# Dense expert gates: one 128-column product per token in place of two of 64, and the second half's gates fetched back in two parts

## The chip, the cores and the metric

The kernel runs on one core of one Trainium2 chip. The metric is the device time of one execution in microseconds (us), taken as the median of several runs; lower is better. Tensors are f32; TensorE (PE) multiplies a stationary 128x128 operand by a moving one and writes into the eight PSUM banks of 512 f32 columns; VectorE (DVE), ScalarE (ACT) and GpSimd (POOL) do the rest, and SyncE (SP) issues most loads.

## The reference, cut to what matters

Two transformer blocks; the change lies in the last part, the layer of 16,384 experts addressed by product keys (128 first keys times 128 second keys). Each of 512 tokens picks 16 experts for each of 8 heads:

```
sc, idx = top_k(query . sub_keys)            # 16 first and 16 second keys per head
top_sc, pos = top_k(sums of pairs)           # 16 pairs per head -> expert = first*128 + second
gate = softmax(top_sc)
act  = gelu(u_tab[expert] . h)               # 128 chosen experts per token
y    = sum(gate * act * v_tab[expert])
```

## The kernel before, in words

Of the four blocks of 128 tokens the kernel handles the first two sparsely: each of 256 "rows" is an indirect DMA on POOL's queue (L1279) that fetches one expert's up and down vector (8 KB) for each of 128 tokens, 1 MB in all; DVE takes the dot product (L3549), ACT the gelu and the weight (L2679, L2681), and DVE adds the weighted down vector (L3561). A row's place is fetched again only once the row before it in that place was added.

The other 256 tokens are handled densely, over all experts. There are 256 *items* of 512 KB, loaded by SP into four buffers (`raws`, L1081), each as soon as the item four before is done. An up item j (`up_unit`, L2017) gives the pre-activations of the 128 experts with second key j, and ACT writes their gelu into `weights[:, j % 64, :]` (`activate`, L2659). A down item m (`down_unit`, L2032) multiplies `weights[:, m % 64, :]`, by then multiplied by the gates, with its down vectors and accumulates in PSUM banks 0 to 3. Only 64 of the 128 second keys fit in `weights` at a time, so the work has two halves. The gate of (token, first key, second key) is found by a scatter done as a matrix product: for a token, `one_first` holds a one-hot row of the first key for each of its 128 (head, choice) entries, `one_second` the one-hot row of the second key times the gate, and their product is the 128x128 gate matrix.

`STEPS` is the order that all engines follow:
- 64 up items (second keys 0 to 63);
- the **gate stage**: 32 steps (`NGATE`) of 8 tokens (`GTOK`). DVE builds `one_first` for 8 tokens (L3512) and `one_second` for four of them with one instruction each (L3516), POOL `one_second` for the other four (L1293); PE makes two products per token (L2044), columns 0 to 63 into one bank and 64 to 127 into the next. DVE multiplies the first bank into `weights` (`gate_weights`, L3528); ACT copies the second to SBUF (`keep_gates`, L2667) and stores it in DRAM (`weights_dram`, L2670), since the second half's gelu values don't exist yet;
- the **mix stage**: 128 items, a down item of the first half and an up item of the second in turn;
- the **back stage**: DVE multiplies the gates fetched back into `weights` (`later_weights`, L3537), 32 times 128x512. SP loads them with `load_gates` (L1091) into `LOADS` = 4 buffers: the first four in the middle of the mix stage, the others behind the item load that ends it, each when a buffer is free. The first down item of the second half waits for all 32 (`down_unit`, L2029);
- the **last stage**: 64 down items.

Rows are spread over the steps by `row_step`: 10 in the gate stage, 120 in the mix stage, 2 in the back stage, 60 in the last. Each engine issues in its program's order: in a step DVE does `one_hots` of it, `gate_weights` of the step before, the addition of the rows of the step before, then the dot products of its own; ACT does the gelu of the step before, `keep_gates` of the step before, then its rows' weights. PE may write a bank once `bank_out` says that it was read.

## Time and profile before

| | us |
|---|---|
| median of 3 runs | 3542.27 |
| range of the runs | 3540.53 to 3545.55 |
| the profiled execution, its own time | 3543.44 |
| its span, first to last instruction | 3541.7 |
| PE busy / DVE busy / POOL busy / ACT busy | 3341.8 / 2201.1 / 1880.8 / 905.8 |

PE's matmul and weight load are separate rows (PE and PEld). Every f32 product appears as two weight loads and two matmuls. The mean granted clock of TensorE over the span is 0.949 of full speed. A row of a timeline gives start, length from the first start to the last end of the group, engine, line, operation and count, and in brackets the idle time before it with what ended it. "DMA share" is the mean busy share of the core's 16 DMA engines; queue q0 is POOL's, q1 is SP's.

### The profile page before, as it was taken

To read this page: it belongs to the slowest core of one execution; us is meant where nothing else is said; L and a number is where in the kernel's file an instruction comes from. 1 tells how busy PE (TensorE), PEld (TensorE's weight loads), DVE (VectorE), ACT (ScalarE), POOL (GpSimd) and SP (SyncE) were. 2 spreads that over 40 slices of the span, in tenths; PEclk is the share of its full clock that TensorE was granted. 3 is DMA by queue.
4 is the path that set the end of the run, shared out by engine and by line. 5 is a ranking of instruction groups with operands and counts; after the bars stand their busy time and mean duration, and the time that the engine had idled before them with its cause. 6 is when DMAs were issued, how large, how long until landed. Compare 5 with 4: busy or idle time off the path is not lost.

```text
span 3541.7 us, 39029 instructions
## 1 busy us (share of the span) xinstructions
PE 3341.8 (94%) x14292; PEld 2517.4 (71%) x14292; DVE 2201.1 (62%) x3653; ACT 905.8 (26%) x1952; POOL 1880.8 (53%) x1072
## 2 busy tenths in 40 slices
PE   8999999999999999999999999997899988996898
PEld 5779778886857888688776677766899655663433
DVE  5764443337674333589367767899655896566765
ACT  4564431112174111201123413222211221111111
POOL 3544269997104999698775472222577333342420
PEclk9999999999999999999999999999755999998999
DMA  4430022222302222234312127777622899999996
GB/s 161 166 130 1 24 86 102 97 107 83 131 36 72 95 95 95 83 110 143 104 72 95 37 89 300 279 267 279 220 86 103 333 364 417 381 412 375 384 417 268
DMA packets 117764, 628.72 MB, mean 178 GB/s; under 512 B 12889, under 2 KB 13017, under 8 KB 62041
## 3 DMA queue, kind: packets, MB, share of 16 engines
q1 hardware_dynamic: 72496, 343.07, 26.3%
q0 software_dynamic: 36864, 268.45, 19.4%
q10 hardware_dynamic: 8232, 14.95, 1.1%
q8 instruction: 103, 1.69, 0.2%
q14 instruction: 69, 0.56, 0.0%
HBM read 607.55 MB, written 18.87 MB: 177 GB/s over the span
## 4 chain that ended last, share of the span: by engine, by line
PE 72%; DVE 11%; DMA 10%; issue 3%; ACT 2%; POOL 1%; DVEq 0%; ACTq 0%; POOLq 0%; SPq 0%
PE bank L1447 13%; PE bank L1448 13%; PE bank L1449 13%; PE bank L2017 6%; PE bank L2032 6%; PE bank L2044 6%; DMA residual<-in_peer_ut 5%; DMA residual<-in_peer_vd 3%; DVE arena L3549 1%; PE bank L1893 1%; PE bank L1875 1%; PE bank L1761 1%; DVE squares L3381 1%; PE bank L1394 1%; PE bank L1639 1%
## 5 line engine op out<-in xcount | busy, mean ns | idle before, releaser
L1449 PE MATMUL bank<-split_arena 128*128 128x512 f32 x1776 | 696.3, 392 | 0.0
L1279 POOL DMA_INDIRECT arena<-in_peer_uv,rstd x181 | 261.8, 1446 | 624.3 <-DVE weight_ring L3561 325.3
L1186 POOL TENSOR_TENSOR split_arena<-weight_ring,ones 128x1024 fp32r<-128x1024 f32 x204 | 505.1, 2476 | 155.1 <-PE bank L1449 99.2
L1447 PE MATMUL bank<-split_arena 128*128 128x512 f32 x1392 | 546.6, 393 | 5.4 <-DVE split_normed L2908 2.5
L1448 PE MATMUL bank<-split_arena 128*128 128x512 f32 x1392 | 542.5, 390 | 0.0
L2017 PE MATMUL bank<-normed,residual 128*128 128x256 f32 x2048 | 483.3, 392 | 55.1 <-ACT arena L2659 37.1
L1188 POOL TENSOR_TENSOR split_arena<-weight_ring,split_arena 128x1024 fp32r<-128x1024 f32 x204 | 520.1, 2550 | 16.0
L2032 PE MATMUL bank<-residual,arena 128*128 128x512 f32 x1024 | 468.7, 604 | 47.3 <-DVE arena L3537 41.4
L2017 PEld LDWEIGHTS bank<-normed,residual 128*128 128x128 f32 x2048 | 395.9, 196 | 162.0 <-issue 59.8
L2032 PEld LDWEIGHTS bank<-residual,arena 128*128 128x128 f32 x1024 | 190.4, 192 | 288.2 <-issue 238.6
L1449 PEld LDWEIGHTS bank<-split_arena 128*128 128x128 f32 x1776 | 334.4, 188 | 73.1
L1155 POOL TENSOR_TENSOR split_arena<-weight_ring,split_arena 128x1024 fp32r<-128x1024 f32 x54 | 129.5, 2407 | 401.9 <-ACT split_arena L2170 349.9
L1447 PEld LDWEIGHTS bank<-split_arena 128*128 128x128 f32 x1392 | 261.9, 188 | 68.0 <-issue 8.1
L1448 PEld LDWEIGHTS bank<-split_arena 128*128 128x128 f32 x1392 | 261.7, 188 | 55.1 <-issue 1.2
L3549 DVE CUSTOM_DVE_ANT_0 arena<-arena,branch 128x1024 f32<-128x1024 f32 x181 | 220.2, 1220 | 30.9 <-DMA arena<-in_peer_uv,rstd 30.7
L1447 PE MATMUL bank<-split_normed,split_arena 128*128 128x512 f32 x560 | 223.5, 399 | 4.9 <-DVE split_arena L3185 3.8
L1448 PE MATMUL bank<-split_normed,split_arena 128*128 128x512 f32 x560 | 222.1, 397 | 0.0
L2679 ACT ACTIVATE row_gelu<-dots 128x1 f32<-128x1 f32 x256 | 51.5, 201 | 648.1 <-DVE dots L3549 648.0
L1279 POOL DMA_INDIRECT weight_ring<-in_peer_uv,rstd x75 | 103.0, 1373 | 171.3 <-DVE branch L3561 96.5
L1293 POOL TENSOR_SCALAR branch<-arena,masks 128x128 f32<-128x128 f32 x128 | 152.4, 1201 | 55.5 <-PE bank L2044 50.6
L3561 DVE SCALAR_TENSOR_TENSOR branch<-arena,row_gelu,branch 128x1024 f32<-128x1024 f32 x84 | 107.8, 1283 | 105.3 <-ACT row_gelu L2681 104.8
L2211 ACT ACTIVATE squares<-squares 128x512 f32<-128x512 f32 x64 | 40.4, 632 | 486.6 <-DVE squares L2823 486.6
(508 smaller groups left out, 5476.9 us busy)
## 6 DMA issues: line engine op xcount, KB each, us to landing
residual<-in_peer_ut SPq DMA_DIRECT2D x128, 512.0 KB, 7.5
residual<-in_peer_vd SPq DMA_DIRECT2D x128, 512.0 KB, 11.0
weight_ring<-in_w_up SPq DMA_DIRECT2D x32, 1024.0 KB, 4.8
weight_ring<-in_w_down SPq DMA_DIRECT2D x32, 1024.0 KB, 4.8
weight_ring<-in_w_in SPq DMA_DIRECT2D x32, 1024.0 KB, 4.9
weight_ring<-in_ada_w SPq DMA_DIRECT2D x24, 1024.0 KB, 4.8
weight_ring<-in_w_in_a SPq DMA_DIRECT2D x12, 1024.0 KB, 6.6
weight_ring<-in_w_out SPq DMA_DIRECT2D x12, 1024.0 KB, 6.9
```

Source lines behind the costliest of these rows:

```text
L1155: pool.tensor_tensor(lo, raw(u)[:, :, h * P:(h + 1) * P], f32(hi), ALU.subtract).then_inc(split_ready, 1)
L1186: pool.tensor_tensor(hi, part, bc_mid(ones[:], DT), ALU.mult).then_inc(split_hi, 1)
L1188: pool.tensor_tensor(lo, part, f32(hi), ALU.subtract).then_inc(split_ready, 1)
L1279: pool.indirect_dma_start(row_places[i][0], None, a["peer_uv"], bass.IndirectOffsetOnAxis(ap=experts[n][:, c:c + 1], axis=0)).then_inc(row ...
L1293: m = pool.tensor_scalar(one_second[q % 2][:, x, :], iota_key, index_t[b][:, 1, at:at + 1], index_t[b][:, 2, at:at + 1], ALU.is_equal, ALU ...
L1447: pe.matmul(psum[t.bank][:], hi, a_hi[k], start=first, stop=False)
L1448: pe.matmul(psum[t.bank][:], lo, a_hi[k], start=False, stop=False)
L1449: return pe.matmul(psum[t.bank][:], hi, a_lo[k], start=False, stop=last)
L2017: m = pe.matmul(psum[t.bank][:, 0:DENSE], blk(raws[n % RAWS], k), H[:, k, DENSE:], start=k == 0, stop=k == DT - 1)
L2032: x = pe.matmul(psum[2 * b + c][:], blk(weights[:, m % WHALF, :], b), raws[n % RAWS][:, 512 * c:512 * (c + 1)], start=m == 0, stop=m == NK ...
L2044: m = pe.matmul(psum[t.bank][:, x * WHALF:(x + 1) * WHALF], one_first[q % 2][:, x, :], one_second[q % 2][:, x, half * WHALF:(half + 1) * W ...
L3549: dve.tensor_tensor_reduce(row, row, h_tok[:, n, :], 1.0, 0.0, ALU.mult, ALU.add, dots[:, r % RING8:r % RING8 + 1]).then_inc(row_dot, 1)
```

## The change

All 128 second keys of a token come from one product of 128 columns, so a bank now holds four tokens, both halves. `one_second` is built as plain one-hots by one DVE instruction for six tokens (POOL keeps two, still multiplied by the gate); ACT then multiplies the six by their gates in place (`scale_ones`) before PE uses them. ACT's `keep_gates` copies the second half out of both banks and signals `gate_read`; DVE's `gate_weights` waits for that and multiplies the first half out of both banks. The stored gates come back in two parts of 32 second keys: part 0 is loaded with one load per item from item 132 on and multiplied in by DVE in 32 steps of the mix stage (`back_at`), part 1 in the back stage. There are eight buffers of half the size.

```diff
-LOADS = 4
+LOADS = 8
+BACKS = 2
+BACK_J = WHALF // BACKS
+POOL_HOT = 2
...
+        BACK_ITEM = WHALF + WHALF + 4
+        back_at = {MIX_AT + WHALF + 3 + q: q for q in range(NGATE)}
...
-            def load_gates(q):
+            def load_gates(n):
-                if q == 0:
+                part, q = divmod(n, NGATE)
+                if n == 0:
                     full(sp, gate_tiles[NGATE - 1][0])
                     for x in gate_stored:
                         sp.wait_ge(x, 16 * NGATE // 2)
-                if q >= LOADS:
-                    sp.wait_ge(gate_used, q - LOADS + 1)
-                sp.dma_start(gate_back[q % LOADS], weights_dram[q]).then_inc(gate_landed[q % LOADS], 16)
+                if n >= LOADS:
+                    sp.wait_ge(gate_used, n - LOADS + 1)
+                sp.dma_start(gate_back[n % LOADS], weights_dram[q][:, part * BACK_J * GTOK:(part + 1) * BACK_J * GTOK]).then_inc(
+                    gate_landed[n % LOADS], 16)
...
-                elif n == 2 * WHALF:
-                    for q in range(LOADS):
-                        load_gates(q)
+                elif BACK_ITEM <= n < BACK_ITEM + NGATE + LOADS:
+                    load_gates(n - BACK_ITEM)
                 elif n == 3 * WHALF + RAWS - 1:
-                    for q in range(LOADS, NGATE):
+                    for q in range(NGATE + LOADS, BACKS * NGATE):
                         load_gates(q)
                     sp.dma_start(H[:, :, :], x_dram).then_inc(x_back, 16)
...
-                for x in range(GTOK // 2, GTOK):
+                for x in range(GTOK - POOL_HOT, GTOK):
...
-                    pe.wait_ge(gate_used, NGATE)
+                    pe.wait_ge(gate_used, BACKS * NGATE)
...
+                pe.wait_ge(scaled_hot, q + 1)
...
                 for x in range(GTOK):
-                    for half, t in enumerate(gate_tiles[q]):
-                        m = pe.matmul(psum[t.bank][:, x * WHALF:(x + 1) * WHALF], one_first[q % 2][:, x, :],
-                                      one_second[q % 2][:, x, half * WHALF:(half + 1) * WHALF], start=True, stop=True)
+                    t = gate_tiles[q][2 * x // GTOK]
+                    m = pe.matmul(blk(psum[t.bank], x % (GTOK // 2)), one_first[q % 2][:, x, :], one_second[q % 2][:, x, :],
+                                  start=True, stop=True)
...
             def keep_gates(q):
-                t = gate_tiles[q][1]
                 if q >= 2:
                     act.wait_ge(gate_stored[q % 2], 16 * (q // 2))
-                full(act, t)
-                act.activation(gate_out[q % 2].rearrange("p (j t) -> p j t", t=GTOK), psum[t.bank][:].rearrange("p (t j) -> p j t", t=GTOK),
-                               ACT.Copy).then_inc(bank_out[t.bank], 1)
-                have(act, t)
+                full(act, gate_tiles[q][0])
+                dst = gate_out[q % 2].rearrange("p (j t) -> p j t", t=GTOK)
+                for x, t in enumerate(gate_tiles[q]):
+                    m = act.activation(dst[:, :, x * GTOK // 2:(x + 1) * GTOK // 2],
+                                       psum[t.bank][:].rearrange("p (t j) -> p j t", j=NKEY)[:, WHALF:, :], ACT.Copy)
+                m.then_inc(gate_read, 1)
+                act.wait_ge(gate_read, q + 1)
                 act.dma_start(weights_dram[q], gate_out[q % 2]).then_inc(gate_stored[q % 2], 16)
+            def scale_ones(q):
+                b, t = divmod(q, NGATE // 2)
+                act.wait_ge(vector_hot, q + 1)
+                for x in range(GTOK - POOL_HOT):
+                    one = one_second[q % 2][:, x, :]
+                    m = act.activation(one, one, ACT.Copy, scale=index_t[b][:, 2, GTOK * t + x:GTOK * t + x + 1])
+                m.then_inc(scaled_hot, 1)
...
+                if kind == "gate":
+                    scale_ones(v)
                 if s and STEPS[s - 1][0] == "gate":
                     keep_gates(STEPS[s - 1][1])
...
-                for x in range(GTOK // 2):
-                    at = GTOK * t + x
-                    m = dve.tensor_scalar(one_second[q % 2][:, x, :], iota_key, index_t[b][:, 1, at:at + 1],
-                                          index_t[b][:, 2, at:at + 1], ALU.is_equal, ALU.mult)
-                m.then_inc(vector_hot, 1)
+                own = GTOK - POOL_HOT
+                dve.tensor_tensor(one_second[q % 2][:, 0:own, :], bc_mid(iota_key, own), bc_last(index_t[b][:, 1, GTOK * t:GTOK * t + own], NKEY),
+                                  ALU.is_equal).then_inc(vector_hot, 1)
...
-                w = weights[:, :, GTOK * q:GTOK * (q + 1)]
-                full(dve, t)
-                dve.tensor_tensor(w, w, psum[t.bank][:].rearrange("p (t j) -> p j t", t=GTOK), ALU.mult).then_inc(bank_out[t.bank], 1)
+                dve.wait_ge(gate_read, q + 1)
+                for x, t in enumerate(gate_tiles[q]):
+                    w = weights[:, :, GTOK * q + x * GTOK // 2:GTOK * q + (x + 1) * GTOK // 2]
+                    dve.tensor_tensor(w, w, psum[t.bank][:].rearrange("p (t j) -> p j t", j=NKEY)[:, 0:WHALF, :],
+                                      ALU.mult).then_inc(bank_out[t.bank], 1)
...
-                w = weights[:, :, GTOK * q:GTOK * (q + 1)]
-                dve.wait_ge(gate_landed[q % LOADS], 16 * (q // LOADS + 1))
-                dve.tensor_tensor(w, w, gate_back[q % LOADS].rearrange("p (j t) -> p j t", t=GTOK), ALU.mult).then_inc(gate_used, 1)
+                w = weights[:, part * BACK_J:(part + 1) * BACK_J, GTOK * q:GTOK * (q + 1)]
+                dve.wait_ge(gate_landed[n % LOADS], 16 * (n // LOADS + 1))
+                dve.tensor_tensor(w, w, gate_back[n % LOADS].rearrange("p (j t) -> p j t", t=GTOK), ALU.mult).then_inc(gate_used, 1)
...
                 for r in rows_at[s]:
                     dot_row(r)
+                if s in back_at:
+                    later_weights(0, back_at[s])
```

## Rows read from the trace of the kernel before

**Rows 1.** The page: PE's granted clock in tenths, 40 slices of 88.5 us

```profile
PEclk9999999999999999999999999999755999998999
```

**Rows 2.** Busy time by stretch: start:end, length, engines, clock, DMA share, GB/s

```profile
2531.00:2749.00 218.00, 218.00 (x1024) 218.00 (x1023) 110.46 (x209) 22.98 (x49) 157.76 (x136) 0.50 0.28 96
...
3012.00:3018.00 6.00, 6.00 (x14) 4.85 (x15) 0.00 (x0) 0.00 (x0) 0.00 (x0) 0.50 0.65 264
3018.00:3024.00 6.00, 6.00 (x21) 3.74 (x21) 3.76 (x5) 1.27 (x5) 1.68 (x1) 0.99 0.43 123
...
3060.00:3240.00 180.00, 177.16 (x584) 107.64 (x584) 110.52 (x136) 29.77 (x117) 74.00 (x47) 1.00 1.02 414
3245.00:3286.00 41.00, 0.00 (x0) 0.00 (x0) 25.70 (x39) 1.23 (x5) 2.28 (x2) 0.52 0.88 313
3286.00:3296.00 10.00, 9.88 (x18) 4.30 (x19) 8.35 (x12) 1.99 (x8) 3.92 (x3) 0.74 0.45 162
3296.00:3500.00 204.00, 201.09 (x489) 85.02 (x488) 142.17 (x173) 30.49 (x117) 61.67 (x52) 1.00 1.01 415
```

**Rows 3.** Timeline of one gate step, and the stage's first and last instruction

```profile
2523.87 1.22 DVE L3512 TENSOR_TENSOR mem_keys<-arena,masks 128x1024 f32<-128x1024 f32 x1 [3.19 <-ACT masks L2143]
...
2564.83 7.03 PE L2044 MATMUL bank<-branch,mem_values 128*128 128x64 f32 x32
...
2565.68 1.22 DVE L3512 TENSOR_TENSOR mem_keys<-arena,masks 128x1024 f32<-128x1024 f32 x1
...
2566.82 1.11 DVE L3516 TENSOR_SCALAR branch<-arena,masks 128x128 f32<-128x128 f32 x4
...
2750.23 6.16 PE L2032 MATMUL bank<-residual,arena 128*128 128x512 f32 x8 [0.87 <-DVE arena L3528]
```

**Rows 4.** Like instructions (timeline, groups, two lines' instructions with min/median/max ns, gate stage)

```profile
2517.29 1.05 PE L1949 MATMUL bank<-mem_values,arena 128*128 128x128 f32 x8
2124.75 2.45 ACT L2586 ACTIVATE normed<-normed,ada 128x128 f32<-128x128 f32 x8
2558.86 1.28 DVE L3561 SCALAR_TENSOR_TENSOR weight_ring<-weight_ring,row_gelu 128x1024 f32<-128x1024 f32 x1
2572.51 1.22 DVE L3549 CUSTOM_DVE_ANT_0 arena<-arena,branch 128x1024 f32<-128x1024 f32 x1
L2659 ACT ACTIVATE arena<-bank 128x256 f32<-128x256 f32 x128 | 47.9, 375 | 217.6 <-PE bank L2017 217.5
L3451 DVE TENSOR_TENSOR weight_ring<-iota,rstd 128x256 f32<-128x256 f32 x4 | 1.7, 424 | 0.1
L1293 POOL TENSOR_SCALAR branch<-arena,masks x124: 780/795/2862, 2531.8 to 2739.2; 128x128 f32<-128x128 f32 x124
L3549 DVE DVE_READ_ACCUMULATOR2_ANT dots<- x10: 78/82/84, 2527.2 to 2723.8; 128x1 f32 x10
```

**Rows 5.** Mix stage: longest wait; item loads before, first and after the four gate loads

```profile
3012.00 6.70 PE L2017 MATMUL bank<-normed,residual 128*128 128x256 f32 x16 [12.53 <-DMA residual<-in_peer_ut]
DMA to landing us min/median/max: 3.6/11.3/11.3
2984.88 0.82 SPq L1091 DMA_DIRECT2D mem_keys<-gate_half  x2
DMA to landing us min/median/max: 19.0/22.6/23.8
```

**Rows 6.** DMA queues between 3060 and 3240 us: packets, MB, share of 16 engines

```profile
q0 software_dynamic: 6671, 48.62, 65.1%
q1 hardware_dynamic: 7097, 25.86, 36.2%
```

**Rows 7.** Timeline of the back stage: start, first wait, first products after

```profile
3245.32 1.29 DVE L3537 TENSOR_TENSOR arena<-arena,mem_keys 128x512 f32<-128x512 f32 x2 [5.88 <-ACT arena L2659]
...
3252.58 1.32 DVE L3537 TENSOR_TENSOR arena<-arena,mem_keys 128x512 f32<-128x512 f32 x2 [3.61 <-DMA mem_keys<-gate_half]
...
3286.12 14.32 PE L2032 MATMUL bank<-residual,arena 128*128 128x512 f32 x27 [41.37 <-DVE arena L3537]
```

More of the change, by code:

```diff
@@ L785, in build @@
         gate_out = [work_a, work_b]
-        gate_back = [k[:, i * SEQ:(i + 1) * SEQ] for k in keys_t for i in range(2)]
+        gate_back = [k[:, i * UNIT_N:(i + 1) * UNIT_N] for k in keys_t for i in range(4)]
         index_t = [masks[:, 3 * i:3 * i + 3, :] for i in range(2)]
@@ L907, in build @@
         pool_hot = sem("pool_one_hot_ready")
+        scaled_hot = sem("one_hot_scaled")
+        gate_read = sem("gate_banks_copied")
         gate_stored = [sem(f"gate_half_stored{i}") for i in range(2)]
@@ L2025, in down_unit @@
                         free(pe, t)
-                    for t, _ in gate_tiles[NGATE - 2:]:
+                    for t in gate_tiles[NGATE - 2] + gate_tiles[NGATE - 1]:
                         have(pe, t)
                 elif m == WHALF:
-                    pe.wait_ge(gate_used, NGATE)
+                    pe.wait_ge(gate_used, BACKS * NGATE)
                 for b in range(2):
@@ L3513, in one_hots @@
                                   ALU.is_equal)
-                for x in range(GTOK // 2):
-                    at = GTOK * t + x
-                    m = dve.tensor_scalar(one_second[q % 2][:, x, :], iota_key, index_t[b][:, 1, at:at + 1],
-                                          index_t[b][:, 2, at:at + 1], ALU.is_equal, ALU.mult)
-                m.then_inc(vector_hot, 1)
+                own = GTOK - POOL_HOT
+                dve.tensor_tensor(one_second[q % 2][:, 0:own, :], bc_mid(iota_key, own), bc_last(index_t[b][:, 1, GTOK * t:GTOK * t + own], NKEY),
+                                  ALU.is_equal).then_inc(vector_hot, 1)
             def gate_weights(q):
-                t = gate_tiles[q][0]
                 if q == 0:
@@ L3525, in gate_weights, with later_weights @@
                         have(dve, x)
-                w = weights[:, :, GTOK * q:GTOK * (q + 1)]
-                full(dve, t)
-                dve.tensor_tensor(w, w, psum[t.bank][:].rearrange("p (t j) -> p j t", t=GTOK), ALU.mult).then_inc(bank_out[t.bank], 1)
-            def later_weights(q):
+                dve.wait_ge(gate_read, q + 1)
[3 more added lines that the diff above has]
+                                      ALU.mult).then_inc(bank_out[t.bank], 1)
+            def later_weights(part, q):
+                n = part * NGATE + q
                 if q == 0:
-                    for x in u_tiles[NKEY - 2:]:
+                    end = WHALF + (part + 1) * BACK_J
+                    for x in u_tiles[end - 2:end]:
                         have(dve, x)
-                w = weights[:, :, GTOK * q:GTOK * (q + 1)]
-                dve.wait_ge(gate_landed[q % LOADS], 16 * (q // LOADS + 1))
-                dve.tensor_tensor(w, w, gate_back[q % LOADS].rearrange("p (j t) -> p j t", t=GTOK), ALU.mult).then_inc(gate_used, 1)
+                w = weights[:, part * BACK_J:(part + 1) * BACK_J, GTOK * q:GTOK * (q + 1)]
+                dve.wait_ge(gate_landed[n % LOADS], 16 * (n // LOADS + 1))
+                dve.tensor_tensor(w, w, gate_back[n % LOADS].rearrange("p (j t) -> p j t", t=GTOK), ALU.mult).then_inc(gate_used, 1)
             def dot_row(r):
@@ L3578, in _ @@
                     for q in range(LOADS * v, LOADS * (v + 1)):
-                        later_weights(q)
+                        later_weights(1, q)
                 elif s == MIX_AT:
```

## The prediction

> **What bounds the kernel now.** I read the page first, then busy time by stretch, then timelines of the places that the edit touches. The page shows PE's clock at half for three slices in a row [rows 1]; by stretch that is the gate stage, 218 us with PE busy for all of it at 0.50, the 1.2 GHz level, while DVE and ACT are busy 110 and 23 us [rows 2]. So PE bounds this stage: a step of 8 tokens is 32 matmul records in 7.03 us [rows 3], 0.22 us each, for 64 columns. Eight records of 128 columns take 1.05 us at full clock [rows 4], 0.13 each, so 0.26 at half, the filling of the pipeline included. Twice the columns cost at most a fifth more a record, and there are half as many.
>
> The mix stage is another matter: DMA share 1.02 at 414 GB/s with PE close to busy [rows 2]. The transfers bound it, and likewise the last stage (1.01 at 415 GB/s) [rows 2]. One long hole stands in it: PE waits 12.53 us for an item load [rows 5]. The four gate loads were issued 27 us before; item loads ahead of them landed in 11.3 us, those behind them in up to 23.8 us [rows 5]. The two queues move almost equal numbers of packets, 6671 and 7097, although the gather's are twice as large [rows 6]: they take turns. After the hole DMA has nothing to do for a while: share 0.65 and 0.43 in two stretches of 6 us [rows 2].
>
> The back stage is a plain wait of PE, 41.37 us, for 32 multiplications fed by refills that arrive in bursts; the first refill lands 3.61 us after DVE ran dry [rows 7].
>
> **Gate stage.** From DVE's first one-hots at 2523.87 to the first down product at 2750.23 it takes 226.4 us [rows 3]. After the change PE needs at most 16 records x 0.26 = 4.2 us a step, whichever clock it gets, and no longer bounds. What does is a loop, because DVE's `gate_weights` of step v-1 now waits for ACT's `keep_gates` of v-1, which stands behind ACT's `scale_ones` of v, which waits for DVE's one-hots of v. In order:
> - DVE one-hots: 1.14 us until the next instruction starts for 128x1024 [rows 3], and 0.96 for 128x768, between 1.22 for 1024 [rows 3] and 0.424 for 256 [rows 4]: 2.1 us.
> - ACT scales six rows of 128x128 in place. No such row exists before. Eight instructions 128x128 with a per-partition operand take 2.45 us, so 0.30 each [rows 4]. Lower bound 0.2, upper bound the 0.375 of a 128x256 [rows 4]. I take 0.30, the same shape: 1.8 us.
> - ACT copies two banks' halves, 128x256 at 0.375 each [rows 4], overlapped a little: 0.7 us. The store follows beside DVE's work, 256 KB as before.
> - DVE multiplies two banks, 128x256 at 0.424, overlapped: 0.7 us.
>
> Sum 5.3 us. The PE products of v lie beside DVE's next one-hots: they end 3.9 + 4.2 = 8.1 us after the step began and are wanted at 5.3 + 3.9 = 9.2. POOL makes 64 one-hots in place of 128; its instructions take 0.78 to 2.86 us [rows 4], and two fit while DVE waits for ACT. The ten rows are on DVE's chain now: dot 1.22 and addition 1.28 [rows 4], about 2.3 net, 22 us in all. Start and end: two steps' one-hots, the scaling, first products, copy and multiplication take 9.5 us, then 29 steps of 5.3 = 154, and 9.5 us from the last one-hots to the first down product. 9.5 + 154 + 9.5 + 22 = 195 us: **31 us saved**. Bounds: with overlaps better by 0.3 us a step -40; with durations not overlapping (one-hots 2.2, scaling 6 x 0.39, copies 0.75, products 0.85, four hand-overs of 0.05) 6.3 us a step, nothing to -3.
>
> POOL's instruction takes from 0.78 to 2.86 us, DVE's 128x1024 one 1.22 in both rows [rows 3, 4]. The Trainium skill (SBUF — State Buffer, Who interferes with whom) says that a DVE instruction with two SBUF inputs and a GpSimd one that reads SBUF exclude each other, whoever starts first. By that rule the new 128x768 one-hots could wait for a POOL instruction; in the rows above it is POOL that waits.
>
> **Mix stage.** SP now issues 40 gate loads of 128 KB, one behind each item load from 132 to 171, in place of four of 256 KB. That is 5.24 - 1.05 = 4.2 MB more in a stretch where DMA has no room. At 414 GB/s [rows 2] it costs 10.1 us. The rows are 1 KB where those of before are 2 KB; in the back stage, 313 GB/s at share 0.88 [rows 2], a full share would be 363 GB/s: 11.5 us. No row has 1 KB; I take 12, with 20 as the upper end. In return the burst is gone, and with it DMA's idle time after it: (1.02 - 0.65 + 1.02 - 0.43)/1.02 x 6 = 5.6 us. Net **+6 us**. If instead PE's own hole is what counted, 12.5 us and half of the 6.70 us of products at half clock [rows 5], 3.3 us, would go: 12 - 15.8 = -4 net, the good end.
>
> DVE has 32 new multiplications here, 0.424 each, in a stretch where it is busy 110 of 180 us [rows 2]: hidden. But each waits for its gate load, and behind it on DVE are the row's addition and the next dot, behind that ACT's row weight and gelu, and behind that PE's up product four items on. Counted in steps, the load of gate q goes out when item 128+q is done and holds up item 136+q: seven items lie between, of 3.7 us (584 records in 180 us, 12 an item on the mean) [rows 2], and DVE and ACT need some 3.6 us of it. It may take about 22 us before PE feels it; item loads land in 11.3 [rows 5], the gate one just behind. SP's wait for `gate_used` is older by eight loads and does not block the next item.
>
> **Back stage.** 32 multiplications of 128x256 (0.424) for 32 of twice that; eight are ready, 24 come in three rounds of eight instead of seven rounds of four. Before, the rounds took (3286.1 - 3245.3)/7 = 5.8 us each, with the first at 7.3 [rows 7]. Three rounds: 7.3 + 2 x 5.8 = 19, plus the last multiplications, 21 us. 41.4 - 21 = **20 us saved**; bounds 12 (three rounds of 9) and 27 (paced by DVE alone, 32 x 0.37 plus one row). The residual's return, 2 MB, slides into the last stage, whose first 10 us have a DMA share of 0.45 [rows 2]: hidden there. The last stage itself stays.
>
> Sum: 3543.4 - 31 + 6 - 20 = **3498 us**, against the profiled execution's 3543.4, which is 1.2 above the median shown.
>
> **Rivals.**
> - *The gate loop is longer* (6.3 us a step, no overlap on ACT, or DVE blocked by POOL): -3 in place of -31, 3526 us. For it: the loop has no slack, every 0.1 us costs 3. Against: the 0.30 us row is the same shape. 0.15.
> - *The mix stage gains*: the hole of 15.8 us was worth all of itself and the added bytes fit between gathers: -4 to -10, and the back stage -25: 3479 us. 0.13.
> - *Every gate load costs its turns* (slower). Four loads in a row made PE wait 12.5 us, 3.1 us each [rows 5]. If each of 40 does, that is 125 - 12.5 = 112 us more, and 3543 - 51 + 112 = 3604 us. It decides from 1.6 us a load. Against: turns are lost only while gathers queue up; only 0.94 gather comes per item (120 rows in 128 items), so the queue should drain after a few, and DMA never idles. 
> - *No change within 0.2%*: a load costs between 1.2 and 1.8 us. 0.04.
>
> The forecast has 0.59. A measurement here can tell about 0.2%, 7 us. Faster by more: 0.59 + 0.15 + 0.13 = 0.87; same 0.04; slower 0.09. Range: 3478, the gaining mix stage, to 3528, the long loop; outside lie the two last rivals and some of the ends, 0.2.
>
> **What would show it.** Gate stage about 195 us with DVE starting one-hots every 5.3 us, ACT's scaling near 1.8 us a step, PE idle 1.5 us a step and its clock still half; no PE wait over 4 us in the mix stage, that stage some 6 us longer; the wait of L2032 for DVE near 20 us. I am wrong if ACT's scaled instructions come more than 0.38 apart, if PE waits for items at 3 us a load from item 132 on, or if the refills of the back stage still take seven rounds' time.

## The result and the profile after

The changed kernel takes **3499.53 us** (median of 4 runs, 3496.39 to 3504.54), the kernel before 3542.28 us (4 runs, 3540.53 to 3545.55) beside it: ratio 0.988, 95% interval 0.9862 to 0.9897. The prediction was 3498 us, range 3478 to 3528.

The span of the profiled execution went from 3541.7 to 3502.8 us. By stage, in us (the gate stage runs from DVE's first one-hots to the first down product, the mix stage from there to the end of its last item, the back stage is PE's wait, the last stage the rest):

| | gate | mix | back | last |
|---|---|---|---|---|
| before | 226.4 | 494.5 | 41.4 | 255.6 |
| after | 194.9 | 503.8 | 24.6 | 256.2 |
| predicted change | -31 | +6 | -20 | 0 |
| measured change | -31.5 | +9.3 | -16.8 | +0.6 |

The four measured changes add up to -38.4 us and the spans differ by 38.9, while the medians differ by 42.7: the execution that was profiled is the slowest of the four, 3504.54 us.

PE's granted clock on the page of the kernel after, against [rows 1]:

```profile
PEclk9999999999999999999999999999966999999999
```

The busy time by stretch of the kernel after, which answers to [rows 2]; the columns are the same. The stretches are the middle of the gate stage, part of the mix stage, the back stage, and the last stage:

```profile
2531.00:2710.00 179.00, 99.85 (x489) 93.24 (x489) 104.32 (x148) 74.59 (x252) 75.20 (x73) 0.67 0.31 109
3060.00:3210.00 150.00, 135.92 (x440) 85.18 (x440) 93.28 (x122) 23.63 (x91) 59.17 (x37) 0.95 1.00 400
3223.00:3246.00 23.00, 0.00 (x0) 0.00 (x0) 13.80 (x36) 0.99 (x4) 2.23 (x1) 0.59 0.83 292
3250.00:3500.00 250.00, 236.07 (x573) 100.23 (x571) 162.60 (x200) 41.52 (x151) 64.07 (x54) 0.98 0.90 363
```

In the gate stage no engine is busy for more than 58% of the time now, where PE was busy for all of it. That is what a loop of engines in series looks like: each waits for the one before. One step of it, which answers to [rows 3]:

```profile
2612.02 0.63 ACT L2677 ACTIVATE weight_ring<-bank 128x256 f32<-128x256 f32 x2
...
2612.68 0.75 DVE L3548 TENSOR_TENSOR arena<-arena,bank 128x256 f32<-128x256 f32 x2 [2.46 <-ACT weight_ring L2677]
2613.35 1.22 DVE L3534 TENSOR_TENSOR mem_values<-arena,masks 128x1024 f32<-128x1024 f32 x1
2614.48 0.95 DVE L3537 TENSOR_TENSOR branch<-arena,masks 128x768 f32<-128x768 f32 x1
2615.47 1.86 ACT L2689 ACTIVATE branch<-branch,masks 128x128 f32<-128x128 f32 x6 [2.83 <-DVE branch L3537]
2615.76 1.56 POOL L1301 TENSOR_SCALAR branch<-arena,masks 128x128 f32<-128x128 f32 x2 [3.90 <-PE bank L2053]
2617.24 0.63 ACT L2677 ACTIVATE weight_ring<-bank 128x256 f32<-128x256 f32 x2
...
2617.54 2.02 PE L2053 MATMUL bank<-branch,mem_values 128*128 128x128 f32 x16 [1.89 <-POOL branch L1301]
...
2617.90 0.75 DVE L3548 TENSOR_TENSOR arena<-arena,bank 128x256 f32<-128x256 f32 x2 [2.46 <-ACT weight_ring L2677]
2618.57 1.22 DVE L3534 TENSOR_TENSOR mem_keys<-arena,masks 128x1024 f32<-128x1024 f32 x1
```

From 2613.35 to 2618.57 it is 5.22 us a step: one-hots 2.1, ACT's scaling 1.77 up to its copies, the copies 0.66, DVE's products 0.67 until its next one-hots. DVE stands still for 2.46 us of each step, waiting for ACT's copy. PE's wait is put down to POOL, whose last one-hot ended at 2617.32; ACT's scaling ended at 2617.33, and either would have held PE. Steps whose products run at the full clock, like this one (2.02 us), and steps whose products run at the half clock (3.75 us) both take 5.22 us, so PE does not set the step.

PE's waits in the mix stage, after; the columns are engine, what it wrote, line and what it waited for, then total us, times and the longest. In the kernel before, the wait for `ut` items was one of 12.5 us [rows 5], and two for `vd` items came to 1.0 us:

```profile
PE bank L2040 <- DMA residual<-in_peer_vd: 15.2, 8, 2.8
PE bank L2025 <- ACT arena L2668: 10.4, 5, 4.3
PE bank L2025 <- DMA residual<-in_peer_ut: 7.8, 6, 3.1
PE bank L2040 <- DVE arena L3548: 1.7, 1, 1.7
```

The single long wait became fourteen short ones, 23.0 us in all. (The five waits for ACT, 10.4 us, stand in the kernel before as well.) The longer ones have a price behind them, as this stretch of PE's timeline shows:

```profile
3008.64 3.72 PE L2025 MATMUL bank<-normed,residual 128*128 128x256 f32 x16 [1.36 <-DMA residual<-in_peer_ut]
3014.89 5.40 PE L2040 MATMUL bank<-residual,arena 128*128 128x512 f32 x8 [2.52 <-DMA residual<-in_peer_vd]
```

After the wait of 1.36 us the item's products take 3.72 us, as everywhere. After the wait of 2.52 us they take 5.40 us instead of the 3.6 to 3.7 of their undisturbed neighbours, and the granted clock is 0.68 in them. The six waits of 2.2 to 3.1 us are all followed by an item of 5.2 to 5.4 us, the eight of 1.6 us or less by none.

The back stage, DVE's timeline, which answers to [rows 7]:

```profile
3222.60 1.43 DVE L3560 TENSOR_TENSOR arena<-arena,mem_keys 128x256 f32<-128x256 f32 x4 [5.60 <-ACT arena L2668]
...
3231.38 1.43 DVE L3560 TENSOR_TENSOR arena<-arena,mem_keys 128x256 f32<-128x256 f32 x4 [4.86 <-DMA mem_keys<-gate_half]
...
3235.27 1.43 DVE L3560 TENSOR_TENSOR arena<-arena,mem_keys 128x256 f32<-128x256 f32 x4
...
3239.45 1.43 DVE L3560 TENSOR_TENSOR arena<-arena,mem_keys 128x256 f32<-128x256 f32 x4
...
3245.04 1.43 DVE L3560 TENSOR_TENSOR arena<-arena,mem_values 128x256 f32<-128x256 f32 x4 [4.16 <-DMA mem_values<-gate_half]
```

The first refill comes 8.8 us after the stage's first product (7.3 before [rows 7]), and the last four wait once more, 4.16 us. SyncE issued the residual's 2 MB at 3239.6, so that these last refills share the DMA engines with it and with a gather that POOL issued at 3235.6.

### The profile page after: what moved, and what is told of

Its sections match the earlier page's. It is cut to its first block, busy times and chain, and to the rows that moved or that the text cites. A ratio compares the mean times of both kernels' runs of the same rounds, so it can differ in the third digit from the quotient of the medians.

```text
span 3502.8 us, 38167 instructions
## 1 busy us (share of the span) xinstructions
PE 3229.5 (92%) x13780; PEld 2400.8 (69%) x13780; DVE 2197.4 (63%) x3621; ACT 964.7 (28%) x2176; POOL 1797.9 (51%) x1008
## 3 DMA queue, kind: packets, MB, share of 16 engines
q0 software_dynamic: 36864, 268.45, 19.6%
## 4 chain that ended last, share of the span: by engine, by line
PE 66%; DVE 15%; DMA 10%; ACT 4%; issue 4%; POOL 2%; DVEq 0%; ACTq 0%; POOLq 0%; SPq 0%
PE bank L1455 13%; PE bank L1456 13%; PE bank L1457 13%; PE bank L2040 6%; PE bank L2025 5%; DMA residual<-in_peer_vd 5%; DMA residual<-in_peer_ut 3%; DVE arena L3572 2%; ACT branch L2689 1%; DVE weight_ring L3584 1%; DVE squares L3403 1%; PE bank L1901 1%; PE bank L1883 1%; PE bank L1769 1%; PE bank L1402 1%
## 5 line engine op out<-in xcount | busy, mean ns | idle before, releaser
L2040 PE MATMUL bank<-residual,arena 128*128 128x512 f32 x1024 | 475.5, 611 | 45.4 <-DVE arena L3560 24.6
L1455 PEld LDWEIGHTS bank<-split_arena 128*128 128x128 f32 x1392 | 261.6, 188 | 67.9 <-issue 8.6
L1456 PEld LDWEIGHTS bank<-split_arena 128*128 128x128 f32 x1392 | 261.6, 188 | 54.6 <-issue 1.5
L3220 DVE SCALAR_TENSOR_TENSOR bank<-arena,vector_columns,bank 128x512 f32<-128x512 f32 x232 | 153.3, 753 | 0.1
L2845 DVE SCALAR_TENSOR_TENSOR squares<-bank,rstd 128x512 f32<-128x512 f32 x64 | 44.1, 692 | 170.4 <-PE bank L1457 154.2
```

Source lines behind the costliest of these rows:

```text
L1455: pe.matmul(psum[t.bank][:], hi, a_hi[k], start=first, stop=False)
L1456: pe.matmul(psum[t.bank][:], lo, a_hi[k], start=False, stop=False)
L2040: x = pe.matmul(psum[2 * b + c][:], blk(weights[:, m % WHALF, :], b), raws[n % RAWS][:, 512 * c:512 * (c + 1)], start=m == 0, stop=m == NK ...
L3220: m = dve.scalar_tensor_tensor(acc[i] if j < CONV_B - 1 else Y[:, k + i, :], glu[:, k + i, j:j + SEQ], vcol("conv_w_2", j * DT + k + i), a ...
```

## The experiments

Two theories were tested for each half of the change. The gate stage: a loop through DVE, ACT and DVE's `gate_weights`, or an engine's own work. The mix stage: the returned bytes, or the turns that every extra transfer takes in the queue.

**e1_gate_only** keeps the new gate stage and returns the gates as before.

```diff
-LOADS = 8
+LOADS = 4
-                        later_weights(1, q)
+                        later_weights(q)
-                if s in back_at:
-                    later_weights(0, back_at[s])
...
```

> The changed gate stage with the old return of the gates (four buffers, 2 KB rows, all multiplied in the back stage). Theory: the parts add up, so this has the gate stage of after (195 us where before has 226), the mix stage of before with its burst of four gate loads and a wait of PE of some 12 us (494 us), and the back stage's wait of 41 us: 3542 - 31 = 3511 us. Rival (the parts hang together, a shorter gate stage leaves DMA or DVE work that the later stages pay for): above 3518 us.

Measured: 3507.61 us (3504.68 to 3516.31), ratio 0.9912 [0.9894, 0.9931]. Stages 193.1, 492.9, 39.7, 255.2.

**e2_return_only** keeps the old gate stage and returns the gates in two parts.

```diff
-LOADS = 4
+LOADS = 8
+BACKS = 2
+BACK_J = WHALF // BACKS
...
+                if s in back_at:
+                    later_weights(0, back_at[s])
```

> The old gate stage with the new return in two parts. Theory: gate stage 226 us, mix stage 9 us longer than before, back stage's wait 25 us in place of 41, so 3542 + 9 - 17 = 3534 us, within 4. Rival (the two parts of the return bring nothing on balance, what the back stage saves the mix stage pays): 3540 us or above.

Measured: 3532.14 us (10 runs, 3530.28 to 3543.24), ratio 0.9976 [0.9966, 0.9986]. Stages 226.4, 499.9, 23.9, 255.8. The two parts of the change are worth 34.5 and 10.0 us against 3542.09 beside them, 44.5 together, and the whole change 42.7: they add up within what the runs can tell, and both kernels are the theory's case.

**e3_weights_later** takes DVE's `gate_weights` two steps behind the one-hots instead of one. DVE then no longer waits for the copy that stands behind the scaling of its own newest one-hots.

```diff
-                    if v:
-                        gate_weights(v - 1)
+                    if v > 1:
+                        gate_weights(v - 2)
...
                 elif s == MIX_AT:
+                    gate_weights(NGATE - 2)
                     gate_weights(NGATE - 1)
```

> DVE multiplies the gates into the weights two steps behind the one-hots in place of one, so that it no longer waits for an ACT copy that stands behind the scaling of the same step. Theory (the bound of the gate stage is the loop DVE, ACT, DVE of 2.1 + 1.9 + 0.7 + 0.7 us): the loop is open, the next bound is the path one-hots, scaling, products over two steps, (2.1 + 1.9 + 3.7) / 2 = 3.9 us a step at PE's half clock and 3.0 at its full one, so the gate stage falls from 195 to some 150 us and the kernel to 3455 to 3465 us. Rival (DVE's own work or PE's products bound the stage): no change, 5.2 us a step, 3499 us.

Measured: 3454.98 us (3450.76 to 3458.47), ratio 0.9758 [0.9742, 0.9774]: 44.6 us below the kernel after. The gate stage takes 147.1 us instead of 194.9. The loop was the bound, and it is gone. The size came out as expected, the next bound did not: it isn't the theory's path of one-hots, scaling and products, but POOL. The first row is the stretch of the gate stage, the second POOL's one-hots in it (min/median/max ns); the third is the same for the kernel after:

```profile
2531.00:2660.00 129.00, 84.95 (x475) 80.64 (x475) 99.47 (x141) 74.77 (x247) 119.91 (x69) 0.74 0.39 139
```

```profile
L1301 POOL TENSOR_SCALAR branch<-arena,masks x62: 780/1842/3454, 2532.0 to 2666.2; 128x128 f32<-128x128 f32 x62
```

```profile
L1301 POOL TENSOR_SCALAR branch<-arena,masks x60: 780/789/2633, 2530.5 to 2699.7; 128x128 f32<-128x128 f32 x60
```

POOL is busy 119.9 of 129 us. Its 62 instructions are the same work as before, but they take 1.84 us at the median instead of 0.79. DVE, busy 77% of the time instead of 58%, leaves them fewer pauses; that this is the cause is argued from the three kernels that differ in it (here, after, e10). That POOL bounds the stage is shown by e10, which halves its work.

**e7_keep_first** (a single run) puts ACT's copies of the step before ahead of its scaling.

```diff
-                if kind == "gate":
-                    scale_ones(v)
                 if s and STEPS[s - 1][0] == "gate":
                     keep_gates(STEPS[s - 1][1])
+                if kind == "gate":
+                    scale_ones(v)
```

> ACT copies the gates of the step before ahead of the scaling of this one. Theory (whatever stands between DVE's one-hots and the next wait sets the step): DVE no longer waits for the copy, but the scaling now waits for PE's products of the step before, and the step becomes scaling 1.9, products 2.0 to 3.7 by the clock, copy 0.7 and hand-overs 0.3, 4.9 to 6.6 us; at the half clock the gate stage is some 30 us longer than after's 195. Rival (the order on ACT doesn't matter, its busy time does): 5.2 us a step as in after, 195 us.

Measured: 3523.55 us, gate stage 222.5 us. The timeline of one step:

```profile
2600.04 0.66 ACT L2677 ACTIVATE weight_ring<-bank 128x256 f32<-128x256 f32 x2 [4.06 <-PE bank L2053]
...
2601.10 1.86 ACT L2689 ACTIVATE branch<-branch,masks 128x128 f32<-128x128 f32 x6 [0.40 <-ACT weight_ring L2677]
...
2603.18 3.75 PE L2053 MATMUL bank<-branch,mem_values 128*128 128x128 f32 x16 [3.23 <-issue]
2607.03 0.38 ACT L2677 ACTIVATE weight_ring<-bank 128x256 f32<-128x256 f32 x1 [4.06 <-PE bank L2053]
```

From copy to copy a step is 6.99 us: copy, scaling and products now stand in series, with ACT idle for 4.06 us while PE works. Most steps of its PE run at the half clock (3.75 us). The order in which one engine takes its two tasks is worth 27.6 us of this stage, the theory's "some 30".

**e4_act_queue** lets ScalarE issue the first 40 gate loads on its own queue; nothing else moves.

```diff
-                elif BACK_ITEM <= n < BACK_ITEM + NGATE + LOADS:
-                    load_gates(n - BACK_ITEM)
...
+                if BACK_ITEM - 3 <= s - NGATE < BACK_ITEM - 3 + NGATE + LOADS:
+                    load_gates(s - NGATE - BACK_ITEM + 3)
...
+                act.dma_start(gate_back[n % LOADS], weights_dram[q][:, part * BACK_J * GTOK:(part + 1) * BACK_J * GTOK]).then_inc(
+                    gate_landed[n % LOADS], 16)
```

> The 40 gate loads of the mix stage are issued by ACT on its own DMA queue, at the same places; the rest is as in after. Theory (in SP's queue each gate packet costs the items behind it a turn of the large gather packets): PE's waits of 2 to 3 us for items between items 132 and 171, some 24 us in all, shrink to under 1 us each, its clock no longer dips, and the mix stage is 3 to 8 us shorter: 3492 to 3497 us. Rival (only the added bytes count, DMA being busy all the time): the waits are spread otherwise but the mix stage stays within 2 us of 504, 3499 us.

Measured: 3490.55 us (3487.12 to 3499.08), ratio 0.9853 [0.9836, 0.9869], 9.0 us below the kernel after, though the two intervals overlap, and 1.5 us below the theory's range. Mix stage 496.5 us instead of 503.8. One profile each would be thin evidence, but other kernels below and above have the same loads in this stage: five that issue them on SP's queue (after, e2, e3, e7, e13) take 503.8, 499.9, 499.4, 496.3 and 503.2 us, mean 500.5, and five that issue them on ACT's (e4, e8, e10, e11, e12) 496.5, 496.1, 495.9, 494.5 and 492.6, mean 495.1. The second queue is worth some 5 us. PE's waits in the mix stage:

```profile
PE bank L2033 <- DMA residual<-in_peer_vd: 8.6, 22, 1.1
PE bank L2018 <- DMA residual<-in_peer_ut: 7.8, 20, 0.9
```

The waits for items are 16.4 us in all, in 42 pieces, none over 1.1 us, and between 2960 and 3140 us the granted clock is 1.00 where it is 0.95 in the kernel after. The queues of the same stretch, packets, MB and share of 16 engines, first of the kernel after and then of this one:

```profile
q0 software_dynamic: 6346, 46.16, 61.8%
q1 hardware_dynamic: 11758, 27.51, 39.2%
```

```profile
q0 software_dynamic: 6377, 46.46, 61.6%
q1 hardware_dynamic: 6425, 23.39, 32.1%
q10 hardware_dynamic: 5760, 5.25, 8.4%
```

ACT's 5760 packets are simply all that its 40 loads have, 144 each, and in the kernel after SP's one queue moved 11758 packets beside the gather's 6346. So the prediction's reading of [rows 6], that the two queues take turns because their counts are almost equal, fails in the kernel after. The rule of the Trainium skill that the prediction named (DMA: Bandwidth & Descriptors, Queues, rings and completion order) says the engines go round the queues packet by packet; these counts neither show nor refute it. That item loads come in smaller lumps when the gate loads have a queue of their own is measured. Why they do, that on one queue they stand behind the gate loads' small packets and on two they don't, is argued.

**e5_no_first_part** leaves out the load and the multiplication of part 0, so that 32 of the 128 second keys keep a weight without its gate.

```diff
-                elif BACK_ITEM <= n < BACK_ITEM + NGATE + LOADS:
+                elif BACK_ITEM + NGATE <= n < BACK_ITEM + NGATE + LOADS:
...
-                if s in back_at:
-                    later_weights(0, back_at[s])
```

> As after, but part 0 of the gates is neither loaded nor multiplied in: 32 of the 40 gate loads of the mix stage and 32 of DVE's multiplications are left out, so half of the second half's experts go without their gate. It prices them. Theory (they cost what after's mix stage is longer, plus what their absence frees of DMA): mix stage 504 - 12 = 490 to 494 us, the PE waits for items over 1.5 us gone, 3487 to 3490 us in all. Rival (the stage is longer for another reason, its start or DVE's new order): it stays above 500 us.

Measured: 3482.11 us (3479.1 to 3484.39), ratio 0.9825 [0.9809, 0.9842], 17.4 us below the kernel after. Mix stage 484.2 us, PE's waits for items 4.5 us in all, one of them 2.5. Part 0 costs more than the theory said: the stage is 6 us below its 490 and the time 5 us below its 3487. This run splits the mix stage's term: against before, the hole is worth 494.5 - 484.2 = 10.3 us; against after, part 0 costs 503.8 - 484.2 = 19.6 us, and the difference is the 9.3 that was measured. With e1, which has the same burst as before and a mix stage of 492.9 us, the hole is worth 8.7.

**e6_small_rows** halves the rows of part 0's loads, so that the same number of packets moves half the bytes; the other half of each buffer holds what was there before, so that 16 of the second keys get a wrong gate.

```diff
+                width = BACK_J * GTOK // 2 if part == 0 else BACK_J * GTOK
+                at = part * BACK_J * GTOK
-                sp.dma_start(gate_back[n % LOADS], weights_dram[q][:, part * BACK_J * GTOK:(part + 1) * BACK_J * GTOK]).then_inc(
-                    gate_landed[n % LOADS], 16)
+                sp.dma_start(gate_back[n % LOADS][:, 0:width], weights_dram[q][:, at:at + width]).then_inc(gate_landed[n % LOADS], 16)
```

> As after, but each load of part 0 fetches only the first 128 of 256 floats of each of its 128 rows: as many packets, half the bytes; what is multiplied in for the rest is left over data. Theory (turns: what an item loses to a gate load is one turn of the gather's packets for each gate packet, whatever its size): PE's waits for items stay at 20 us or more, with several of 2 to 3 us, and the mix stage stays at 502 to 505 us. Rival (bytes): the waits fall by half or more of what the change added, under 18 us, and the stage to 498 us or below.

Measured: 3493.2 us (3487.44 to 3493.55), ratio 0.9854 [0.9838, 0.9871]. Mix stage 495.9 us, PE's waits for items 18.0 us in all, the longest 2.9: the rival's stage (498 us or below), with the waits at the rival's bound of 18. Halving part 0's bytes bought 7.9 of its 19.6 us with the packets unchanged, and 6.3 of 17.4 us by the medians. But the five mix stages with part 0 on SP's queue differ by 7.5 us among themselves in their one profile each, as much as this difference. Against their mean, 500.5, part 0 costs 16.3 us and half of its bytes 4.6. So the bytes account for 9 to 16 us and whatever goes by the packet for 4 to 7: bytes are at least half of the price, and the split is no sharper than that. The prediction's 12 for part 0 was low, and its upper end of 20 held.

**e8_later_and_act** puts e3 and e4 together.

> The multiplication two steps behind together with the gate loads on ACT's queue. If the two are independent they add: 3455 - 9 = 3446 us, within 5; gate stage 147 us, mix stage 493 to 496 us. If the gain of one was the same time as that of the other (a shorter gate stage leaving the mix stage more to catch up), 3450 us or above.

Measured: 3449.56 us (3446.51 to 3452.82), ratio 0.9739 [0.9723, 0.9756]. Stages 143.2, 496.1, 23.2, 256.1. The mix stage keeps what e4 gave; of the total, 5.4 us more than e3. The time is within the theory's 5 us and 0.4 short of the rival's 3450, so this run doesn't decide between them.

**e10_pool_one** is e8 with one one-hot on POOL.

```diff
-POOL_HOT = 2
+POOL_HOT = 1
```

> As e8_later_and_act, with POOL making one one-hot of the eight in a step instead of two; VectorE compares and ScalarE scales seven. Theory: with the products two steps behind, GpSimd is what sets the step (in e8_later_and_act the gate stage takes 143.2 us, and in e3_weights_later GpSimd is busy 131 of 142 us, its instructions stretched by VectorE's). Halving its work leaves ScalarE the longest, about 7 x 0.30 + 2 x 0.63 = 3.4 us a step against 3.8: gate stage 128 to 136 us, time about 3439 us. Rival: the step is still a ring of one-hots, scaling, matmuls and freed banks, which gets 0.3 us longer with the seventh scaling: gate stage 148 to 153 us, time about 3457 us.

Measured: **3427.06 us** (3425.34 to 3427.56), ratio 0.9668 [0.9652, 0.9684]. Gate stage 126.7 us, below the theory's 128 to 136; the time is 12 us below its 3439. The gate stage holds 16.5 of the 22.5 us by which the median fell from e8. Its middle:

```profile
2531.00:2640.00 109.00, 67.54 (x463) 62.47 (x462) 104.67 (x145) 82.53 (x279) 89.51 (x40) 0.90 0.48 161
```

DVE is busy 104.7 of 109 us: the fourth bound of this stage in a row, after PE [rows 2], the loop and POOL. The theory had named ACT as the next one; it is busy 82.5. POOL's one instruction a step takes 2.75 us at the median now, and PE waited for it once, 5.5 us.

**e11_residual_later** is e8 with the residual's load two items later.

```diff
                         load_gates(q)
+                elif n == 3 * WHALF + RAWS + 1:
                     sp.dma_start(H[:, :, :], x_dram).then_inc(x_back, 16)
```

> As e8_later_and_act, with the load of the saved residual (2 MB) issued two items later, so that it does not stand on SyncE's queue among the last refills of the returned gates. Theory: the last refills are late (VectorE waits 4.2 us for one in the kernel after the change) because they share the DMA engines with the residual's load: the back stage's wait falls from 23.2 us to 18 to 20 us, the last stage stays at 256 us, time about 3446 us. Rival: those refills wait for the items' loads and the gathers ahead of them in any case, and each is issued before the residual's load, so nothing moves: wait 22.5 to 24 us, time 3449 to 3450 us.

Measured: 3456.56 us (3455.38 to 3459.68), ratio 0.9755 [0.9739, 0.9772]. The back stage's wait is 24.9 us, not shorter, and the last stage takes 261.6 us, 5.5 more, with one wait of 3.0 us for an item. The theory about the last refills fell: they aren't late because of the residual. The traces have another candidate, which no run tests. In e11, e8, e3 and after alike POOL issues a gather of 1 MB 0.1 us before the last eight refills (here 3180.76 us against 3180.84), and the last four are usable only 6 to 8 us after the first of them was issued; the eight refills before, with no gather issued in the 12 us ahead of them, were usable within 3.6 us. The gate stage of e11 took 151.6 us against 143.2 in e8, though nothing of it differs; while POOL bounds that stage, its length varies from profile to profile (147.1 in e3), and the 7.0 us between the medians of e11 and e8 aren't to be put down to the residual alone.

**e13_split_alone** is the kernel after with PE's wait split: the last stage's first 32 down items use part 0 alone.

```diff
-        GAIN_AT, X_FIRST_AT = LAST_AT + 3, LAST_AT + 8
+        GAIN_AT, X_FIRST_AT = LAST_AT + 18, LAST_AT + 22
...
-                elif n == 3 * WHALF + RAWS - 1:
-                    for q in range(NGATE + LOADS, BACKS * NGATE):
-                        load_gates(q)
+                if n == 3 * WHALF + RAWS - 1:
                     sp.dma_start(H[:, :, :], x_dram).then_inc(x_back, 16)
+                if 0 <= n - (3 * WHALF + RAWS - 1) < (NGATE - LOADS) // 2:
+                    for x in range(2):
+                        load_gates(NGATE + LOADS + 2 * (n - (3 * WHALF + RAWS - 1)) + x)
...
                 elif m == WHALF:
+                    pe.wait_ge(gate_used, NGATE)
+                elif m == WHALF + BACK_J:
                     pe.wait_ge(gate_used, BACKS * NGATE)
...
-                elif kind == "back":
-                    for q in range(LOADS * v, LOADS * (v + 1)):
-                        later_weights(1, q)
+                elif 0 <= s - LAST_AT < NGATE // 2:
+                    for x in range(2):
+                        later_weights(1, 2 * (s - LAST_AT) + x)
```

> The kernel after the change, with the wait for the returned gates split: the first down item of the last stage waits for part 0 alone, the item 32 later for part 1. Part 1 is multiplied two tokens' groups a step in the first 16 steps of the last stage, its last 24 loads are issued two an item, and the small products of the residual and the gains stand 15 and 14 steps later, since their buffers are now in use until then. Theory: nothing but part 1 holds TensorE in the back stage, so its wait falls from 24.6 us to under 3 us, and the last stage grows by 2 to 6 us for loads among the items as the mix stage did: time 3478 to 3485 us. Rival: VectorE's rows or the loads among the items hold the last stage instead (the products of part 1 add 17 us to VectorE, the loads 8 MB at about 400 GB/s, 10 us of them beside items): last stage 268 us or more, time 3490 us or more.

Measured: 3494.8 us (3488.89 to 3499.58), ratio 0.9858 [0.9838, 0.9878], 4.7 us below the kernel after with intervals that overlap. The wait for part 1 is gone as the theory said, but PE's timeline shows what took its place, and the stretch by engines (columns as in [rows 2]) shows why:

```profile
3224.64 14.99 PE L2043 MATMUL bank<-residual,arena 128*128 128x512 f32 x32
3252.68 5.16 PE L2043 MATMUL bank<-residual,arena 128*128 128x512 f32 x8 [13.05 <-DMA residual<-in_peer_vd]
3259.86 0.70 PE L2043 MATMUL bank<-residual,arena 128*128 128x512 f32 x1 [2.02 <-DMA residual<-in_peer_vd]
```

```profile
3225.00:3275.00 50.00, 33.60 (x72) 13.51 (x70) 35.19 (x55) 5.98 (x25) 17.71 (x12) 0.86 1.02 418
```

PE runs on for four items and then waits 13.05 us for the next one's load, with DMA at share 1.02 and 418 GB/s. The back stage had been hiding transfers that had to be made anyway: the rows' gathers (12.4 of the 20.9 MB of these 50 us), items, refills and the residual. From the end of the mix stage (3224.6 us) to the end it takes 272.8 us, 8.0 less than the 280.8 of after; of 24.6 us of wait a third was to be had. That is the rival's case (last stage of 268 us or more). The trace shows a second cause that no run separates from the first: SP issues in order, an item load stands behind two refills, and between 3222 and 3275 us SP stood still for 17.1 us, 5.6 at the longest, until DVE had freed a refill's buffer. (Part 1 is 32 loads of 128 KB, 4.2 MB, not the expectation's 8.)

**e12_wait_split** is the same edit on e10.

> The same edit on e10_pool_one (gate products two steps behind, first loads on ScalarE's queue, one one-hot on GpSimd). Theory: e10_pool_one's 3427.1 us less its wait of 24.6 us plus the same 2 to 6 us in the last stage: 3404 to 3409 us. Rival: last stage 268 us or more, time 3415 us or more.

Measured: 3420.88 us (3416.02 to 3425.32), ratio 0.9659 [0.9643, 0.9675]. The theory's 3404 to 3409 us is missed and the rival's case came (3415 or more): from the end of the mix stage to the end it takes 275.3 us, 5.5 less than the 280.8 of e10. Again one long wait for an item, in PE's timeline:

```profile
3166.65 6.65 PE L2036 MATMUL bank<-residual,arena 128*128 128x512 f32 x8 [12.89 <-DMA residual<-in_peer_vd]
```

It has the lowest median of all, 120 us below the kernel before beside it and 79 below the kernel after, but what the split adds to e10 (6.2 us) lies within overlapping intervals.

## Why the prediction was right

The time came out 1.5 us from the forecast, and the case that came true is the one it gave 0.59. The mechanisms were the ones named: PE freed, the loop as the new bound, fewer rounds in the back stage, part 0 paid for in the mix stage. That it is 1.5 us and not 6 is luck: in the profiled execution the mix and back stages were each some 3 us worse than forecast, and that execution, 3504.54 us, is 6.5 from it. The steps one by one:

- **The step of the gate stage.** 5.3 us forecast, 5.22 measured; ACT's scaling 1.8 forecast, 1.86 for six; copies and products as forecast. The stage 195 forecast, 194.9 measured; a pair of steps with one row in it takes 12.78 us, 2.3 over two plain steps, as forecast. PE's records, put at 0.26 us at most at the half clock, took 0.23 (16 in 3.75 us), hardly more than the 0.22 of half the columns [rows 3]: that is where the change frees PE. That the loop and not an engine's work sets it is shown by e3, which opens it (-47.8 us), and by e7, which closes it elsewhere (+27.6 us). The prediction saw that the wait for `gate_read` ties DVE to ACT's newest scaling; it did not ask what the stage would cost without that tie.
- **PE's clock there.** Forecast to stay at its half level, measured 0.67, so this sign was wrong: PE is idle for 44% of the stretch, and some steps run at the full level (16 records in 2.02 us, granted clock 1.00), some at half (3.75 us at 0.50) and some between (3.33 us at 0.57). It cost nothing, since the step is 5.22 us at either level: PE had time to spare, as the sum had assumed.
- **DVE held up by POOL.** The 128x768 one-hots took 0.95 us against 0.96 forecast. It is POOL that is stretched, in every kernel looked into here. The Trainium skill's rule (SBUF — State Buffer, Who interferes with whom) says that the two exclude each other; the trace agrees as far as POOL goes, and of the 32 one-hots none took over 0.96 us in the kernel after and none over 1.05 in e3. By it the loop would have been longer, and this rival (0.15) did not come.
- **The mix stage.** +6 forecast, +9.3 measured in this profile, +5.4 in e2's. Both of its terms were small: the hole is worth 8.7 to 10.3 us, not 5.6 (e5 against e1 and before), and part 0 costs 16.3 to 19.6, not 12 (e5). The step that was off is the hole's price "by DMA's idle time": it came out at 55 to 65% of the 15.8 us that the prediction had counted as PE's own loss. The errors have opposite signs, so the net term stood; that is luck too. The forecast "no PE wait over 4 us" held for items, the longest is 3.1; the one wait of 4.3 us is for ACT and stands in the kernel before as well. The returned multiplications held nobody up: PE's waits for ACT are 10.4 us in both kernels. The price of part 0 lies in the number of waits for items and in the slow clock behind the long ones.
- **Each load costs its turns** (0.09) did not come: part 0's 32 loads cost 16.3 to 19.6 us together, 0.5 to 0.6 us each and not 3.1.
- **The back stage.** -20 forecast, -16.8 measured. Three rounds, as forecast, but of 8.8, 3.9 and 9.8 us in place of 7.3, 5.8 and 5.8. The forecast counted rounds and kept their old length, though DMA was at 313 GB/s there [rows 2] and a round of the new size moves as many bytes as one before (eight times 128 KB, four times 256 KB). The third round is the long one, and why isn't settled: e11 rules out the residual's load, and the gather issued just before is untested.
- **The last stage** was forecast to stay, and it did.

## What to carry to other kernels

When a stage stops being bound by an engine, look for the loop that takes over: add the durations along the waits of one step, and if they make the whole period, moving one consumer a step later (e3, a few lines) can be worth as much as the change itself (44.6 us here, against 42.7). A wait at a barrier can hide transfers that are due in any case; before removing it, look at the DMA share around it, and expect back only what that leaves free. Small loads in a queue of large ones cost more than their bytes: part 0's 4.2 MB are 10.1 us at 414 GB/s and cost 16.3 us by the mean of five profiles on SP's queue, 10.9 on ACT's. In e4 the second queue spread the waits so that the clock didn't fall.

## What the runs showed of the hardware

POOL's 128x128 compare takes 0.79 us at the median where DVE is busy 58% of the time (the kernel after), 1.84 where it is busy 77% (e3) and 2.75 at 96% (e10); DVE's 128x1024 one-hots stay at 1.22 us in all three, its 128x768 ones at 0.95 in the first two. Work given to POOL beside a busy DVE cost up to three and a half times its price here. And the same bytes cost PE more when they come in lumps: waits of 2.2 to 3.1 us are followed by products at a lower clock (granted 0.68, 5.40 us an item instead of 3.7), and in e4, whose waits are none above 1.1 us, the clock was 1.00 over the same stretch.
